# Feed-forward operands split in high and low part at the producer, reloaded by transfers alone

## The reference, cut to what matters

```
h = rms_norm(x, ln_ffn_pre)                              # (1024, 1024) per sequence, D_FF = 2816
f = (jax.nn.silu(h @ w_gate) * (h @ w_up)) @ w_down
x = x + rms_norm(f, ln_ffn_post)
```

## Time and profile before

| | |
|---|---|
| time, median of 3 runs | 2670.71 us (2670.15 to 2676.42) |
| the profiled execution's own time | 2673.0 us |
| its span, first to last instruction | 2671.2 us |
| mean granted TensorE clock | 0.958 |
| first and last feed-forward matmul | 1026.8 and 2375.2 us |

### The profile page before, as it was taken

One profiled execution on the slowest core, in us unless ns is written; L12 is line 12 of the kernel. 1 busy time (PEld: TensorE's weight loads), 2 busy tenths in 40 slices (PEclk: granted clock), 3 DMA queues, 4 the chain that ended last, 5 costly groups with the idle time before them and its releaser, 6 DMA issues. The chain is left out here.

```text
span 2671.2 us, 32707 instructions
## 1 busy us (share of the span) xinstructions
PE 2421.9 (91%) x11528; PEld 1998.9 (75%) x11528; DVE 1618.9 (61%) x1824; ACT 1097.0 (41%) x1617; POOL 869.9 (33%) x549
## 2 busy tenths in 40 slices
PE   7989999398999955999999988799999999869898
PEld 6878878387887844888888767688888887757777
DVE  6678854366887426544446778765555677764632
ACT  4368854333886433232223433333332343423231
POOL 0034420201453033443444245443445435430300
PEclk9999999699999977999999999899999999989999
DMA  4000033500000356333335432754265443345422
GB/s 137 16 32 17 1 121 96 164 32 16 25 9 34 135 146 194 117 119 103 98 96 174 141 130 87 235 152 126 85 200 186 168 158 129 115 163 195 124 72 77
DMA packets 270864, 295.50 MB, mean 111 GB/s; under 512 B 14320, under 2 KB 211824, under 8 KB 270576
## 3 DMA queue, kind: packets, MB, share of 16 engines
q1 hardware_dynamic: 270128, 291.33, 34.4%
q0 software_dynamic: 576, 2.10, 0.2%
HBM read 208.98 MB, written 84.41 MB: 110 GB/s over the span
## 5 line engine op out<-in xcount | busy, mean ns | idle before, releaser
L1115 PE MATMUL ps<-reg,ring 128*128 128x512 f32 x5544 | 1290.3, 395 | 107.4 <-DVE ring L1768 57.9
L1115 PEld LDWEIGHTS ps<-reg,ring 128*128 128x128 f32 x5544 | 1056.4, 191 | 340.9 <-DVE ring L1768 69.5
L1768 DVE TENSOR_TENSOR ring<-wraw,ring 128x1024 fp32r<-128x1024 f32 (+2 forms) x152 | 218.1, 1436 | 183.3 <-ACT ring L1211 180.4
L1211 ACT ACTIVATE ring<-wraw 128x1024 fp32r<-128x1024 f32 (+2 forms) x152 | 143.7, 945 | 403.7 <-PE ps L1115 361.3
L877 PE MATMUL ps<-win,ht 128*128 128x512 f32 (+1 forms) x1152 | 233.9, 361 | 41.7 <-DVE win L1624 41.4
L877 PEld LDWEIGHTS ps<-win,ht 128*128 128x128 f32 x1152 | 190.5, 192 | 73.5 <-DVE win L1624 44.8
L1211 ACT ACTIVATE ring<-ws 128x1024 fp32r<-128x1024 f32 (+2 forms) x114 | 107.7, 945 | 330.7 <-PE ps L1115 319.0
L1777 DVE TENSOR_TENSOR reg<-stg,reg 128x1024 fp32r<-128x1024 f32 (+1 forms) x126 | 192.0, 1524 | 49.3 <-ACT reg L1211 41.8
L877 PE MATMUL ps<-x2r,gsp 128*128 128x512 f32 x768 | 184.0, 399 | 24.8 <-DVE x2r L1969 18.4
L1708 DVE TENSOR_TENSOR pt<-ps,pt 128x512 fp32r<-128x512 f32 x256 | 172.2, 686 | 48.0 <-ACT pt L1211 45.7
L877 PEld LDWEIGHTS ps<-x2r,gsp 128*128 128x128 f32 x768 | 147.8, 193 | 58.9 <-issue 14.8
(11 more groups left out here) (194 smaller groups left out, 2907.7 us busy)
## 6 DMA issues: line engine op xcount, KB each, us to landing
ff_forms<-ev SPq DMA_DIRECT2D x66, 512.0 KB, 2.7
stg<-ff_forms SPq DMA_DIRECT2D x56, 512.0 KB, 5.9
wraw<-in_w_gate SPq DMA_DIRECT2D x44, 512.0 KB, 6.2
wraw<-in_w_up SPq DMA_DIRECT2D x44, 512.0 KB, 7.0
wraw<-in_w_down SPq DMA_DIRECT2D x48, 384.0 KB, 5.2
stg<-h_forms SPq DMA_DIRECT2D x28, 512.0 KB, 4.6
stg<-ff_forms SPq DMA_DIRECT2D x42, 256.0 KB, 3.0
xs_a<-in_x SPq DMA_DIRECT2D x18, 512.0 KB, 3.5
```

The source lines that it names most:

```text
L1115: last = nc.tensor.matmul(ps[:, 2 * chain + m, :], ring[:, st % 3, a, m, k * P:(k + 1) * P], reg[:, k, i, e, :], start=OPENS[i] and k == 0 ...
L1211: copy = lambda out, src, **k: nc.scalar.activation(out, src, ACT.Copy, **k)
L1768: V.tensor_tensor(ring_block(u, st, 1), weight_source(u, i), f(ring_block(u, st, 0)), ALU.subtract).then_inc(S["w_split"], 1)
```

## The change

Activations are split where they are made. When a form pair stands in SBUF, ACT copies it to a new three-slot tile `fhi` (`ff_hi`, four copies a gate unit) and DVE subtracts (`ff_lo`, four subtractions), three of them in place. High and low parts go to DRAM apart: 3.5 MB a gate unit in eight transfers where 1.75 MB went in four. For a down part one transfer per form (1536 KB, or 1024 KB in the last part) brings both parts from DRAM straight into `reg`, once the step that last read that place is done; PE waits on the transfer. `fill_hi` and `fill_lo` stay for the two gate stages only.

Weights come in halves of a unit over three places of `wraw`: the first half two units ahead at step 5, the second half one unit ahead at step 1. The POOL sums are reordered so that the first needs the first half alone, and products 2 and 3 swap their sources.

```diff
@@ def encoder_layer
-    fff_d = nc.dram_tensor("ff_forms", (NSEQ, P, NP, NJ, CH), F32, kind="Internal").ap()
+    fff_d = nc.dram_tensor("ff_forms", (NSEQ, P, NP, NJ, 2, CH), F32, kind="Internal").ap()
...
-        wraw = sb(two, "wraw", [P, 2, 8 * CH])
+        wraw = sb(two, "wraw", [P, 3, 4 * CH])
+        fhi = sb(two, "fhi", [P, 3, 2, CH], F32R)
...
@@ sync: def fill_in
+                if part:
+                    k0, nk = DPART0[part - 1], DPART[part - 1]
+                    sp.wait_ge(S["step_done"], NP * (FIRST_OF[f] - 1) + i + 1)
+                    sp.dma_start(reg[:, 0:nk, i].rearrange("p k e n -> p k (e n)").bitcast(F32),
+                                 fff_d[s, :, FORM[i], k0:k0 + nk].rearrange("p k e n -> p k (e n)"))\
+                        .then_inc(on(f"op_in{i}"), 16)
+                    return
...
@@ sync: for u in UNITS, for i in range(NP)
                     if u.n and i == 0:
                         if not before.down:
-                            ff_out(before, 1)
-                            ff_out(before, 2)
+                            for r in range(3):
+                                hi_out(before, r)
+                            lo_out(before, 0)
+                            lo_out(before, 1)
...
                     if u.n and i == 1:
                         if not before.down:
-                            ff_out(before, 0)
+                            lo_out(before, 2)
+                            hi_out(before, 3)
+                            hi_out(before, 4)
...
-                    if not u.down and i == 6:
-                        ff_out(u, 3)
+                    if i == 1 and u.n + 1 < NU:
+                        weights_in(UNITS[u.n + 1], 1)
                     if i == 5 and u.n + 2 < NU:
-                        weights_in(UNITS[u.n + 2])
+                        weights_in(UNITS[u.n + 2], 0)
...
@@ tensor: def product
                 if FIRST_OF[u.fill] == u.n:
-                    pe.wait_ge(S["op_split"], NP * u.fill + i + 1)
+                    if u.down:
+                        pe.wait_ge(*at_least(f"op_in{i}", 16 * (4 * u.seq + u.part + 1)))
+                    else:
+                        pe.wait_ge(S["op_split"], NP * u.seq + i + 1)
...
@@ scalar
+            def ff_hi(u, r):
+                n = NG * u.seq + u.j
+                use = HI_USES * n + r
+                slot = use % 3
+                act.wait_ge(*at_least(f"fhi_out{slot}", hi_landed(slot, use)))
+                if use >= 3 and (use - 3) % HI_USES < 4:
+                    act.wait_ge(S["f_lo"], 4 * ((use - 3) // HI_USES) + (use - 3) % HI_USES + 1)
...
             def middle(u):
...
+                act.wait_ge(S["f_lo"], 4 * (NG * (u.seq + 1) if u.down else NG * u.seq + u.j))
...
                     if st > 0 and not before.down:
                         silu(before, 3)
+                        ff_hi(before, 1)
+                        ff_hi(before, 2)
+                if inside and u.n and i == 1 and not UNITS[u.n - 1].down:
+                    ff_hi(UNITS[u.n - 1], 3)
...
-                for f, n in FIRST_OF.items():
-                    m = st + 4 - NP * n
+                for f in (0, 5):
+                    m = st + 4 - NP * FIRST_OF[f]
...
@@ vector
+            def ff_lo(u, r):
...
+                V.tensor_tensor(out, src, f(flat(fhi[:, slot])), ALU.subtract).then_inc(S["f_lo"], 1)
...
                 if before and not before.down:
                     gated(before, 3)
+                    ff_lo(before, 0)
+                    ff_lo(before, 1)
+                if inside and u.n and i == 1 and not UNITS[u.n - 1].down:
+                    ff_lo(UNITS[u.n - 1], 2)
+                    ff_lo(UNITS[u.n - 1], 3)
```

More of the change, by code:

```diff
@@ L83, in evict_counts @@
     for u in UNITS:
-        counts.append(counts[-1] + (1 if not u.down else (1, 1, 2)[k] if u.part == LASTP else 0))
+        counts.append(counts[-1] + ((0, 1, 1)[k] if not u.down else (1, 1, 2)[k] if u.part == LASTP else 0))
     return counts
@@ L111 @@
 USES = []
-for _f in range(10):
+for _f in (0, 5):
     FILL_USE[_f] = len(USES)
@@ L122, with hi_landed @@
 PIECES = tuple(itertools.accumulate([0] + [kind == "piece" for kind, _ in USES]))
-FILL_PIECE = tuple(itertools.accumulate([0] + [NP * len(fill_pieces(f)) for f in range(10)]))
+FILL_PIECE = {0: 0, 5: NP * len(fill_pieces(0))}
+HI_USES = 5
+def hi_landed(slot, uses):
+    return 16 * len(range(slot, uses, 3))
 class Signal:
@@ L377, in weight_source, with half_landed @@
         def weight_source(u, i):
-            return (raw_block(u, 0, 0), sum_block(u, 1), sum_block(u, 0), raw_block(u, 1, 0),
+            return (raw_block(u, 0, 0), sum_block(u, 1), raw_block(u, 1, 0), sum_block(u, 0),
                     raw_block(u, 0, 1), sum_block(u, 1), raw_block(u, 1, 1))[i]
+        def half_landed(u, m):
+            h = 2 * u.n + m
+            return S[f"raw_w{h % 3}"], sum(16 * (2 if UNITS[v // 2].down else 4) for v in range(h % 3, h + 1, 3))
         def acc_at(u, block):
@@ L494, in _, with weights_in @@
                 stage_end(sp)
[L497 to L501, removed]
-                for nh in range(2):
[L503 to L512, removed]
+            def weights_in(u, m):
+                if u.n:
+                    before = 2 * u.n + m - 3
+                    if before >= 0:
+                        sp.wait_ge(S["w_split"], NP * (before // 2) + (NP if before % 2 else 3))
+                landed = S[f"raw_w{half_at(u, m)}"]
+                for nh in range(2):
+                    if u.down:
+                        r0, c0 = (NJ * m + DPART0[u.part]) * P, (KG * nh + 2 * u.q) * P
+                        sp.dma_start(down_view(u, m)[:, nh, 0:u.nk].rearrange("p k x n -> p k (x n)"),
+                                     w_down[r0:r0 + u.nk * P, c0:c0 + 2 * P].rearrange("(k p) n -> p k n", p=P))\
+                            .then_inc(landed, 16)
+                    else:
+                        c0 = (u.j + NJ * nh) * P
+                        for x, w in enumerate((w_gate, w_up)):
+                            sp.dma_start(gate_view(u, m)[:, nh, x],
+                                         w[m * KG * P:(m + 1) * KG * P, c0:c0 + P]
+                                         .rearrange("(k p) n -> p k n", p=P)).then_inc(landed, 16)
             def stage_in(use, src):
@@ L580, in _ @@
                 sp.wait_ge(S[f"xa_in{b}"], (NSEQ * (NT // 2) + 1) * 16)
-            weights_in(UNITS[0])
+            for m in range(2):
+                weights_in(UNITS[0], m)
             for i in range(2):
                 fill_in(0, i)
-            weights_in(UNITS[1])
+            weights_in(UNITS[1], 0)
             for i in range(2, NP):
@@ L1931, in _ @@
                     norm_step(u, i)
-                for fill, n in FIRST_OF.items():
-                    m = st + 4 - NP * n
+                for fill in (0, 5):
+                    m = st + 4 - NP * FIRST_OF[fill]
                     if 0 <= m < NP:
```

97 lines of the change are left out of this document (70 added, 27 removed).

## The result

The changed kernel takes 2613.44 us (median of 4 runs, 2611.76 to 2615.33) against 2673.52 of the kernel before beside it: ratio 0.9776, 95% interval 0.9759 to 0.9793. The forecast was 2614. The execution that was profiled took 2615.33 us, with a span of 2613.1 for 2671.2.

What follows compares the result with a forecast made beforehand. PE bounds the kernel, delayed mainly by operand fills ahead of DVE's weights; gains 20 + 18 + 11 + 4 + 4 = 57 us off 2673.0 give 2616, median 2614, range 2600 to 2628 (55%).

Steps and rivals of the forecast that it cites:

- The price and the sum: Feed-forward block: 0.2265 us per undisturbed matmul, 91.6 us lost against it; gains 20 + 18 + 11 + 4 + 4 = 57 us.
- the last units: Last units of sequence 1: loss 6.5 to 2.5 us, gain 4.
- the start: Start of the feed-forward block: weights in halves cut the loss from 11.0 to 7 us, gain 4.
- the second gate stage: Gate units of sequence 1: loss 1.0 us before, change costed at nothing; norm steps make it the likelier place for slowing.
- Fills of the down parts: Down stages: 49 copies and 49 subtractions a sequence leave ACT and DVE; losses 23.1 and 21.2 us fall to 3 each.
- only half is won: Down stages: waits at step 5 stay because POOL's accumulation delays DVE; 2640 us; 20% together with transfers near 270 GB/s.
- more is won: Passage's gate fill also runs on time and the gate-to-down border never waits: gain near 78 us, 2593; 13%.
- the passage: Last down part of sequence 0 to the next gate stage: loss 28.8 to 18 us, gain 11.
- The border: Gate to down: 20.7 MB in 62.6 us; at 340 GB/s 61 us, leaving 1 to 2 us lost a sequence.
- transfers set the pace: Border late: 2648 us at 260 GB/s, 2680 at 230; near 270 within a shared 20%, near 240 (no gain) 4%.
- The split at the gate border: Gate unit borders: new copies and subtractions fit within 4 to 8 us of cover, costed at nothing.
- slower: Gate border chain outruns its cover: 3 us at each of 22 borders, 66 in all, 2680; 8%, slower transfers included.

Runs made afterwards that it cites:

- the halves alone: Kernel before with only the weights in halves over three places and POOL's sums in the new order: 2659.43 us, ratio 0.9943.
- The shorter lead: Changed kernel with each down operand transfer issued three steps ahead of its use instead of six: 2634.76 us, ratio 0.9855.
- The traffic run: Changed kernel with a 1 MB DRAM-to-DRAM copy behind each of the 56 operand transfers, on the same queue: 2678.56 us, ratio 1.0024.
- The run with seven passes: Changed kernel with the last low-part subtraction of each gate unit made seven times instead of once: 2762.59 us, ratio 1.0327.
- the runs in the passage: Changed kernel, 8 columns in DVE's low part of the second gate operand (last tile whole): 2609.19 us; in six POOL instructions: 2607.46; in both: 2607.02.
- the run with three passes: Changed kernel with the last low-part subtraction of each gate unit made three times instead of once: 2636.28 us, ratio 0.9869.

## Why the prediction was right, point by point

**The price and the sum.** The loss fell from 91.6 to 30.9 us, 61 for the 57 of the sum; from the start of the first to the end of the last feed-forward matmul it is 1348.8 and 1288.7 us, 60.1 less. The span shows 58.1: the first matmul stands 0.7 us sooner, and the stretch behind the last one is 298.3 us for 295.6 before. In the kernels of the experiments, which run the same program there, it lies between 296 and 300 by their spans and PE's timelines, so this is scatter and no effect of the change. That the forecast lies 0.6 us from the median is luck, for the terms missed both ways: the down stages won 6 us more than stated and the last units 2 more, the start 2 less, and the second gate stage lost 2; the scatter behind took back most of what was over. The mechanism does not hang on this. One of the prediction's rivals was added up wrongly: by its own terms transfers at 230 GB/s come to 2684, and not 2680.

**Fills of the down parts.** The gain was put at 20 and 18 and is 23.1 and 21.0: of the 3 us that were left for each stage 0.2 at most has stayed. The mechanism is shown by the run that cut DVE's work short in the kernel before (44.7 us, ACT's shorter waits for landings included), and by the halves alone, which leave most of the waits in place. The rival *only half is won*, by which POOL's accumulations would make the weights late all the same, is refuted: with the fills gone the waits at step 5 in these stages are gone, but for 0.25 and 0.24 us at steps (17, 5) and (36, 5), where 4.21 and 4.19 stood. The rival *more is won* did not come either, since the passage keeps 17.7 us.

**Transfers.** The border was worked out at 340 GB/s with 1 to 2 us of loss a sequence; it ran at 384 and 399, and PE lost nothing. The shorter lead showed the tight place where the prediction put it, in the units 11 and 30. The traffic run shows that the rival *transfers set the pace* was not out of the way: half as many bytes again, here as copies within DRAM, take the whole gain.

**The split at the gate border.** Predicted: last low part at T + 10.3 to 14.6, weights at T + 14 to 18, cover 4 to 8 us. Measured: T + 14.0 and T + 17.6, cover 4.1. So the longer end held, that of 3.38 us beside POOL, though not in the very instructions: of the three in line the weight subtraction took 2.92 us and the second low part 3.41, and the first low part only 1.21. The Trainium skill's page "SBUF — State Buffer", section "Who interferes with whom", speaks for that end, by its exclusive lock between a DVE instruction with two inputs in SBUF and a GpSimd one that reads SBUF; the trace agrees, with ends 1.08 us apart at the border and with 2.09 us for 8 columns. The rival *slower* was priced at 3 us a border for a chain 3 us too late, 66 in all. The run with seven passes shows 6.35 us for 3.48 of wait, nearly twice that. The price was too low: the prediction says itself that a wait costs more than its length, but priced this one by its length alone.

**The second gate stage** was costed at nothing and lost 2.3 us more than before. Of this two waits are plain, 0.99 us of a token sum behind `g_tile` and the 0.87 for the root that stands at 1881.44 in PE's timeline above. This is the norm steps' place, which the prediction named as the likelier one for trouble.

**The halves.** The start was to gain 4 and gained 1.6 in its window (the wait is 4.35 us for 5.59). In the passage DVE's standing for the store of f went from 8.01 us to 4.08, the 3 us sooner that were worked out from 1 MB and one more, and the wait behind it from 3.56 to 1.26. The passage as a whole came to 17.7 for the 18 predicted, though not by the same rows: the longest wait, 8.03 us, stands ahead of step (18, 6), and was taken as 5.76 and unchanged, and laid to the gate operand's fill as such. So the match is in part luck. By the runs in the passage some 3 us of that wait are DVE's subtractions standing for POOL; the rest is likely the landing of the pieces ahead of them, which no run tried alone. The last units were to keep 2.5 us and keep 0.3, as no operand is split there any more. The halves alone bring 14 us, more than the 4 of the start and their part of the passage; the trace of that run, of an execution of 2653.34 us, shows some 6 us within the units 11 to 16 and 30 to 35, and why weights in halves help there was not tried.

## What to carry to other kernels

Price a wait of PE by the stage's rate before and behind it, not by its length: here a wait of 3.48 us cost 6.35. Work that is moved off the late stage may well cost more engine time than it saves (DVE's total rose by 60 us) if its new place has cover; but count the cover at each kind of border, since one of them (here the border to the down stage, where a buffer's store queues behind loads) has less than the rest. When two engines lock each other out, shortening the instruction that waits may gain nothing (here the wait stayed at 8.41 us): shorten or move the one that holds the lock.

## What the runs showed of the hardware

- A VectorE subtraction of 8 columns took 2.09 us beside a GpSimd instruction and ended with it; of 1024 columns, 3.03 beside and 1.22 without. Its duration in a trace is then GpSimd's.
- A wait of 3.48 us at full clock was followed by 38 matmuls in 11.16 us at a granted clock of 0.76. One of 1.69 us, in the run with three passes, was followed by 168 matmuls in 38.38 us, nearly the undisturbed 38.05.
- Loads and stores mixed ran at 384 to 399 GB/s for 40 us, more than the full stretch of the earlier trace rows showed (372).
